# Differential attention scores from two row halves of TensorE without zero padding, with two pairs of score banks in place of three

## The reference

```python
for i in range(S // Q_BLOCK):                       # 8 blocks of 128 queries
    q0 = i * Q_BLOCK
    end = q0 + Q_BLOCK
    s = einsum('bqhmd,bkhmd->bhmqk', q[:, q0:end], k[:, :end]) * scale   # m: two maps, d = 64
    s = s + bias[None, :, None]
    s = where(rel >= 0, s, -inf)
    p = softmax(s, axis=-1)
    a = p[:, :, 0] - lam * p[:, :, 1]
    outs.append(einsum('bhqk,bkhv->bqhv', a, v[:, :end]))
```

## Time and profile before

| | us |
|---|---|
| median of 3 runs | 2963.22 (2961.62 to 2967.35) |
| the profiled execution | 2965.12 |
| its span, first to last instruction | 2963.2 |
| TensorE busy | 2685.0 (91%) |
| VectorE busy | 1151.2 (39%) |
| ScalarE busy | 840.4 (28%) |
| mean granted TensorE clock | 0.964 of full speed |

### The profile page before, as it was taken

The page is one execution under the profiler, slowest core; times in us unless marked ns, Lnnn a source line. Parts: engine busy times, 40 slices in busy tenths (PEclk is TensorE's granted clock), DMA queues, the critical chain, the costliest instruction groups (busy, mean ns, idle before and its releaser), DMA issues. The chain is left out here.

```text
span 2963.2 us, 30511 instructions
## 1 busy us (share of the span) xinstructions
PE 2685.0 (91%) x12386; PEld 2163.3 (73%) x12386; DVE 1151.2 (39%) x1849; ACT 840.4 (28%) x1469; POOL 122.6 (4%) x159
## 2 busy tenths in 40 slices
PE   8789987769999999999989898876899999999997
PEld 7577775447788888878767687644778888887875
DVE  0543444665422221145554434366451111113554
ACT  0421213543311111134542112155341111113333
POOL 0000000002100000001000000000120000000000
PEclk9898998999999999999999989899999999999998
DMA  4242110002322221144445301100131111113444
GB/s 188 87 168 88 29 57 8 1 22 100 100 71 73 72 70 50 50 137 169 149 151 170 128 22 36 36 1 15 57 114 50 50 50 46 47 50 128 164 144 140
DMA packets 171704, 243.60 MB, mean 82 GB/s; under 512 B 9532, under 2 KB 125101, under 8 KB 170541
## 3 DMA queue, kind: packets, MB, share of 16 engines
q1 hardware_dynamic: 160268, 200.74, 21.1%
q0 software_dynamic: 11296, 40.92, 3.9%
HBM read 224.05 MB, written 17.58 MB: 82 GB/s over the span
## 5 line engine op out<-in xcount | busy, mean ns | idle before, releaser
L1643 PE MATMUL ps<-hT,wsp 128*128 128x512 f32 (+1 forms) x1824 | 720.4, 395 | 9.7 <-DVE hT L1471 6.5
L1645 PE MATMUL ps<-hT,wsp 128*128 128x512 f32 (+1 forms) x1824 | 715.6, 392 | 0.0
L1644 PE MATMUL ps<-hT,wsp 128*128 128x512 f32 (+1 forms) x1824 | 715.3, 392 | 0.0
L1029 DVE TENSOR_TENSOR wsp<-raw,wsp 128x1024 fp32r<-128x1024 f32 (+2 forms) x124 | 148.4, 1197 | 959.1 <-ACT wsp L614 731.5
L1643 PEld LDWEIGHTS ps<-hT,wsp 128*128 128x128 f32 (+1 forms) x1824 | 342.8, 188 | 88.5 <-DVE hT L1471 7.6
L1645 PEld LDWEIGHTS ps<-hT,wsp 128*128 128x128 f32 (+1 forms) x1824 | 341.9, 187 | 76.6 <-issue 2.0
L1644 PEld LDWEIGHTS ps<-hT,wsp 128*128 128x128 f32 (+1 forms) x1824 | 342.5, 188 | 74.4 <-issue 1.4
L614 ACT ACTIVATE wsp<-raw 128x1024 fp32r<-128x1024 f32 x84 | 89.1, 1060 | 767.4 <-PE ps L1645 767.4
L1909 PE MATMUL ps<-hT,asp 128*128 128x512 f32 x1032 | 249.0, 398 | 16.5 <-DVE asp L1548 16.3
L1909 PE MATMUL ps<-wsp,asp 128*128 128x512 f32 x1080 | 257.2, 394 | 4.6 <-DVE asp L1548 4.3
L1909 PEld LDWEIGHTS ps<-hT,asp 128*128 128x128 f32 x1032 | 196.1, 191 | 64.2 <-DVE hT L1540 11.0
(11 more groups left out here) (186 smaller groups left out, 2790.4 us busy)
## 6 DMA issues: line engine op xcount, KB each, us to landing
raw<-in_w_down SPq DMA_DIRECT2D x132, 512.0 KB, 3.5
raw<-in_w_gate_up SPq DMA_DIRECT2D x88, 512.0 KB, 3.8
F<-in_w_mod SPq DMA_DIRECT2D x80, 512.0 KB, 4.6
raw<-in_w_in SPq DMA_DIRECT2D x48, 512.0 KB, 3.7
out_x<-W POOLq DMA_DIRECT2D x32, 512.0 KB, 3.4
W<-out_x POOLq DMA_DIRECT2D x24, 512.0 KB, 5.8
raw<-in_w_out SPq DMA_DIRECT2D x16, 512.0 KB, 3.4
F<-in_w_mod SPq DMA_DIRECT2D x6, 1024.0 KB, 18.6
```

The source lines that it names most:

```text
L1029: v.tensor_tensor(wsp[0:np_, r, 1, 0:w], raw[0:np_, r, 0:w], wsp[0:np_, r, 0, 0:w].bitcast(F32), ALU.subtract).then_inc(s_lo, 1)
L1643: mm(o, a(0), b(0), start=start, stop=False)
L1644: mm(o, a(0), b(1), start=False, stop=False)
L1645: return mm(o, a(1), b(0), start=False, stop=stop)
```

## The change

The scores read queries and keys directly from `F`, map 0 from partitions 0-63 and map 1 from partitions 64-127, without the padded copies. `scores(h, b)` issues both maps of a block, piece by piece and alternately: map 0 into `pair(0)`, map 1 into `pair(1)`. The third pair of banks is no longer used for scores. The scores of block b wait until both exponentials of block b - 1 have read the banks. The factor DK ** -0.5 moves into ScalarE's eviction of the projected queries. `queries`, the memsets, `s_q` and `s_qz` go. In the orders of TensorE, ScalarE and VectorE both maps of block b + 1 are handled in block b; `turned(b, 1)` follows `turned(b, 0)` directly. `hi_out` and `lo_out` of tiles 0 and 1 move behind the last head.

```diff
@@ projection, ScalarE
                     nc.scalar.activation(F[:, bass.ds(i * (2 * S) + (Fq + r * S), S)], pair(r),
-                                         ACT.Copy).then_inc(s_tev, 1)
+                                         ACT.Copy, scale=DK ** -0.5 if i < 2 else 1.0).then_inc(s_tev, 1)
@@ ScalarE
-                def queries(h):
-
-                    act.wait_ge(s_qk, 1 + counts(h)[0])
-                    for m in range(2):
-                        rows = slice(DK * m, DK * m + DK)
-                        last = nc.scalar.activation(Wq[m][rows], F[rows, bass.ds(h * S + Fq, S)],
-                                                    ACT.Copy, scale=DK ** -0.5)
-                    last.then_inc(s_q, 1)
-
-                    nc.scalar.activation(F[:, at:at + n], pair(u % 3)[:, 0:n], ACT.Exp,
+                    nc.scalar.activation(F[:, at:at + n], pair(u % 2)[:, 0:n], ACT.Exp,
@@
                         probs(b, 0)
-                        if 2 * b + 3 < 2 * NT:
-                            exps(h, 2 * b + 3)
+                        if b < NT - 1:
+                            exps(h, 2 * b + 2)
                         elif more:
                             exps(h + 1, 0, groups_before(NT - 1) - groups_before(NT))
                         if b >= 4:
                             probs(b, 1)
-                        if 2 * b + 4 < 2 * NT:
-                            exps(h, 2 * b + 4)
+                        if b < NT - 1:
+                            exps(h, 2 * b + 3)
+                        elif more:
+                            exps(h + 1, 1, groups_before(NT - 1) - groups_before(NT))
                         if b:
                             outs(b - 1)
-                        if b == NT - 2 and more:
-                            queries(h + 1)
-                        if b in (1, 2) and not more:
-                            hi_out(b - 1)
-                    if more:
-                        exps(h + 1, 1)
-                        exps(h + 1, 2)
                     outs(NT - 1)
@@
                 head(HEADS - 1, False)
+                hi_out(0)
+                hi_out(1)
                 hi_out(2)
@@ VectorE
-                v.memset(Wq[0][DK:P], 0.0)
-                v.memset(Wq[1][0:DK], 0.0).then_inc(s_qz, 1)
@@
                         combine(b)
-                        for u in (2 * b + 3, 2 * b + 4):
+                        for u in (2 * b + 2, 2 * b + 3):
                             if u < 2 * NT:
                                 maxes(h, u)
-                        if b in (1, 2) and not more:
-                            lo_out(b - 1)
@@
                 v.tensor_scalar(Wf[4], Wf[3], 1.0 / DV, EPS, ALU.mult, ALU.add).then_inc(s_ams, 1)
+                lo_out(0)
+                lo_out(1)
                 lo_out(2)
@@ TensorE
-                def scores(h, u):
+                def scores(h, b):
                     u0 = l * 64 + h * 16
-                    b, m = u // 2, u % 2
                     n = (b + 1) * P
-                    pe.wait_ge(s_ex, 1 + u0 + max(0, u - 2))
+                    pe.wait_ge(s_ex, 1 + u0 + 2 * b)
                     for c0 in range(0, n, 512):
                         w = min(512, n - c0)
-                        last = mm(pair(u % 3)[:, c0:c0 + w], Wq[m][:, b * P:b * P + P],
-                                  F[:, bass.ds(h * S + (Fk + c0), w)],
-                                  start=True, stop=True)
-                    last.then_inc(s_qk, 1)
+                        for m in range(2):
+                            rows = slice(DK * m, DK * m + DK)
+                            last = mm(pair(m)[:, c0:c0 + w],
+                                      F[rows, Fq + h * S + b * P:Fq + h * S + b * P + P],
+                                      F[rows, Fk + h * S + c0:Fk + h * S + c0 + w],
+                                      start=True, stop=True)
+                            if c0 + w == n:
+                                last.then_inc(s_qk, 1)
@@
-                        if 2 * b + 3 < 2 * NT:
-                            scores(h, 2 * b + 3)
+                        if b < NT - 1:
+                            scores(h, b + 1)
+                        elif more:
+                            scores(h + 1, 0)
                         if b:
                             weighted(b - 1)
                         turned(b, 0)
-                        if 2 * b + 4 < 2 * NT:
-                            scores(h, 2 * b + 4)
-                        elif b == NT - 1 and more:
-                            pe.wait_ge(s_q, l * HEADS + h + 2)
-                            scores(h + 1, 0)
-                            scores(h + 1, 1)
                         if b >= 4:
                             turned(b, 1)
-                    if more:
-                        scores(h + 1, 2)
                     weighted(NT - 1)
```

More of the change, by code:

```diff
@@ L209, in build @@
         Ws = [W[:, 4096 + 256 * i:4352 + 256 * i] for i in range(4)]
-        Wq, Wj = [W[:, 0:1024], W[:, 4096:5120]], W[:, 3072:3200]
+        Wj = W[:, 3072:3200]
         Wf = [W[:, 3200 + 32 * z:3232 + 32 * z] for z in range(6)]
@@ L277, in build @@
         s_oh, s_ol = sem("s_oh"), sem("s_ol")
-        s_qz, s_fin = sem("s_qz"), sem("s_fin")
-        s_q, s_qk, s_ba, s_mx = sem("s_q"), sem("s_qk"), sem("s_ba"), sem("s_mx")
+        s_fin = sem("s_fin")
+        s_qk, s_ba, s_mx = sem("s_qk"), sem("s_ba"), sem("s_mx")
         s_ex, s_rc, s_co, s_ad = sem("s_ex"), sem("s_rc"), sem("s_co"), sem("s_ad")
@@ L820, in hi_out @@
                     act.wait_ge(s_raw[n % 2], raw_in(l, n))
-                    if k < 2:
-                        act.wait_ge(s_q, l * HEADS + HEADS)
-                    elif k < 4:
+                    if k < 4:
                         act.wait_ge(s_qk, 1 + l * 64 + 64)
@@ L860, in head @@
                             probs(b, 1)
-                        if 2 * b + 4 < 2 * NT:
-                            exps(h, 2 * b + 4)
+                        if b < NT - 1:
+                            exps(h, 2 * b + 3)
+                        elif more:
+                            exps(h + 1, 1, groups_before(NT - 1) - groups_before(NT))
                         if b:
                             outs(b - 1)
-                        if b == NT - 2 and more:
-                            queries(h + 1)
-                        if b in (1, 2) and not more:
-                            hi_out(b - 1)
-                    if more:
-                        exps(h + 1, 1)
-                        exps(h + 1, 2)
                     outs(NT - 1)
                 act.wait_ge(s_tev, l * 12 + 12)
[L875 to L878, removed]
+                exps(0, 0)
+                exps(0, 1)
                 for h in range(0, HEADS - 1):
@@ L1326, in maxes @@
                     dve.wait_ge(s_qk, 1 + u0 + u + 1)
-                    near = pair(u % 3)[:, n - w:n]
+                    near = pair(u % 2)[:, n - w:n]
                     v.tensor_tensor(near, near, F[:, bass.ds(h * NEAR + (Fbias + NEAR - w), w)],
@@ L1330, in maxes @@
                     dve.wait_ge(s_ba, u0 + u + 1)
-                    v.tensor_reduce(ast[:, A_NM + u:A_NM + u + 1], pair(u % 3)[:, 0:n], AX.X,
+                    v.tensor_reduce(ast[:, A_NM + u:A_NM + u + 1], pair(u % 2)[:, 0:n], AX.X,
                                     ALU.max, negate=True).then_inc(s_mx, 1)
@@ L1363, in head @@
                         combine(b)
-                        for u in (2 * b + 3, 2 * b + 4):
+                        for u in (2 * b + 2, 2 * b + 3):
                             if u < 2 * NT:
                                 maxes(h, u)
-                        if b in (1, 2) and not more:
-                            lo_out(b - 1)
                     if more:
-                        for u in range(3):
+                        for u in range(2):
                             maxes(h + 1, u)
-                for u in range(3):
+                for u in range(2):
                     maxes(0, u)
@@ L1883, in head @@
                         turned(b, 0)
-                        if 2 * b + 4 < 2 * NT:
-                            scores(h, 2 * b + 4)
-                        elif b == NT - 1 and more:
-                            pe.wait_ge(s_q, l * HEADS + h + 2)
-                            scores(h + 1, 0)
-                            scores(h + 1, 1)
                         if b >= 4:
                             turned(b, 1)
-                    if more:
-                        scores(h + 1, 2)
                     weighted(NT - 1)
-                pe.wait_ge(s_q, l * HEADS + 1)
-                for u in range(3):
-                    scores(0, u)
+                pe.wait_ge(s_tev, l * 12 + 12)
+                scores(0, 0)
                 apart(pe)
```

## The result

The changed kernel takes 3023.36 us (median of 4 runs, 3004.08 to 3040.83) where the kernel before took 2965.28 beside it: slower by 58 us, a ratio of 1.0197, 95% interval [1.0137, 1.0257]. The forecast was 3003, own range 2983 to 3028. The profiled execution took 3040.83 us, span 3038.8, at a mean granted clock of 0.925 (before 0.964). The lines of the page that moved are those of the attention.

What follows compares the result with a forecast made beforehand. The attention stage was taken as a chain through three engines, none full. Start -4.5, loop +2.8, last head -6.8, tail +3.7, clock +30 and -5 give +20.2 us a layer, +40 for both: 3003 us, range 2983 to 3028.

Steps and rivals of the forecast that it cites:

- the terms without the clock: Start, loop, last head, tail and the present falls of the clock (-4.5, +2.8, -6.8, +3.7, -5 us a layer).
- The maps at once: Scores: both row halves overlap fully, so 1024 keys cost 1.72 us for both maps and not 3.44.
- the rival without overlap: Scores of both maps stand in line, 49.5 us a head, 3045 us in all; chance 0.13.
- The loop at the full clock: Attention blocks: 43.0 us a head against 42.3 before, 6.5 at block 5, +2.8 us a layer.
- The start: Start of the attention stage: memsets and query copies no longer hold the first score, -4.5 us a layer.
- The last head: Last head: splits of weight tiles 0 and 1 leave its loop, -6.8 us a layer.
- the -5: Clock falls already present in heads 1 and 2 and at the last head's end, subtracted as -5 us a layer.
- The tail: Behind the last head: TensorE waits for the moved weight splits before the output matmuls, +3.7 us a layer.
- The clock: Attention stage: thinner TensorE work lowers the clock, two fifths of it at the low level, +30 us a layer.
- its own price of 72 us: Attention stage at the low clock throughout: four heads at about 18 us, 72 us a layer.
- The rival "the clock holds": Attention clock stays as now, so the change gains -4.8 us a layer, 2954 us; chance 0.12.
- The rival "low through the whole stage": Attention clock low throughout, +72 us a layer and not +30, 3087 us; chance 0.10.

Runs made afterwards that it cites:

- the second set: The changed kernel, unaltered, measured once more with a second profile: 3015.86 us, ratio 1.0181 against the kernel before.
- the filled kernel: Changed kernel plus one useless 512-column matmul behind the transposes of every block: 2936.61 us, ratio 0.9911 against the kernel before.
- e2: Changed kernel's order and two pairs of banks, but with the zero-padded query copies of the kernel before: 3077.79 us, ratio 1.0384.
- e1: Changed kernel plus one useless 512-column matmul behind the transposes of every block: 2936.61 us, ratio 0.9911.
- e8: Changed kernel with the 512-column filler, weight splits of output tiles 0 and 1 moved into block 7 of the last head: 2928.63 us, ratio 0.9881.
- e9: Changed kernel with the useless 512-column matmul behind the transposes of blocks 0 to 3 of each head only: 2962.71 us, ratio 0.9988.
- e3: Kernel before with its three pairs and order, but row-half scores without copies, and splits behind the last head: 3008.52 us, ratio 1.0146.
- e6: Three-pair kernel with row-half scores and no copies, plus a useless matmul ahead of every weighted sum: 2981.1 us, ratio 1.0046.
- e5: Kernel before plus one useless full-array matmul ahead of the weighted sums: 2963.53 us, ratio 0.9995.
- e7: Changed kernel with the 512-column filler, all score pieces of map 0 issued ahead of those of map 1: 2936.09 us, ratio 0.9904.

## Why the prediction was right

The sign and the cause came out as forecast, and the size within its own range of 2983 to 3028: the medians are 3023 and 3016, above the 3003. The loss is 58 us (51 in the second set) where 40 was forecast, and three of the eight executions (3033 to 3041) lie above the range. A little of it is luck: the terms without the clock add up to -9.8 us a layer, and the filled kernel, which is nearly free of the low clock, has -13.6 ((2936.61 - 2963.75) / 2), so they were too high where the clock's term was too low. Step by step:

- **The maps at once**: right. 1.35 us for eight records of 640 keys; the rival without overlap is excluded (e2 shows what it costs, 3.70 us for 1.99).
- **The loop at the full clock**: right, 42.93 us a head for 43.0, and each block within 0.1 us (e1); from weighted sum to weighted sum at block 5 it is 6.68 us (509.18 to 515.86) for 6.5. That the halved scores and the missing lookahead cancel stands: 42.9 us a head for 42.3 before (42.5, when the eight blocks are read to hundredths).
- **The start**: -4.3 us a layer for -4.5.
- **The last head**: in the filled kernel it takes what the other heads take (42.6 us from its first transposes to its end), where before it took 53.3 (621.58 to 674.9): -10.7, for the -6.8 and the 2 of the -5 that lay there.
- **The tail**: +3.8 us a layer for +3.7, for the reason given; e8 takes it out, 7.5 us in all.
- **The clock**: the right mechanism, too small a term. "I take some two fifths of the TensorE work at the low level, +30 us a layer" is the step that was off. The runs gave 33 to 51, with the stage at 0.66 to 0.74 and not 0.75; by its own price of 72 us for a stage that is low throughout that is 0.46 to 0.71 of the work and not 0.4. The prediction read rightly that the small blocks would be thin. What it left out is the feedback: at the low level block 3 takes 8.0 us and not 5.3, TensorE is idle ahead of its scores for the same waits, and the next block starts low as well, heavy ones too. Blocks 4, 5 and 6 of head 0 take 8.18, 9.85 and 7.73 us in the changed kernel; the same blocks, unfilled too, take 6.14, 6.90 and 5.95 in e9, where the blocks ahead of them had kept the clock. With 44 in place of 30 the sum gives 3033 for the profiled executions, which took 3041 and 3015.
- **The rival "the clock holds"** is excluded for this kernel, and e1 shows where it would have ended: 2937 us with the clock held better than now. The Trainium skill (TensorE: Matmul & The Clock Gate, Why this matters for your kernels) warns of long idle gaps between bursts; no gap in the changed loop is longer than 2.5 us, and the clock fell all the same. The measurement decides.
- **The rival "low through the whole stage"** (3087) is excluded: low for 156.6 of 228.7 us, and no execution over 3041.

One cause is shown for the slowdown: adding useless work to TensorE, and nothing else, makes it a gain of 0.9%. The two hybrids show two ways to the same loss: waits thin TensorE's work when the work is as before (e2, two pairs), and the halving does when the lookahead is as before (e3, three pairs). For each I had expected that the other part was needed, and missed. What stays open is why e6 stays low in a full block; rows, changes of form and the state in which the block begins all differ from the kernel before, and no run parts them.

## What to carry to other kernels

In a chain through several engines, a cut of TensorE's work that isn't on the longest path can cost more than it gives, because the work was what kept its clock up: before making matmuls cheaper, look at the granted clock of the stage and at the busy share of its thinnest blocks. A matmul of no use, laid in a wait that is there anyway, is a cheap test of whether the clock is what was lost, and may be the repair; put it in the thinnest blocks first, and price it, since where it stands in line it can take all that the clock gives back (e5). When work is moved out of a loop to its end, look at which engine then waits with nothing in hand.

## What the hardware showed unexpectedly

- TensorE stayed at the low level through a block of 11.9 us in which it was busy without a pause, over half of it score matmuls on 64 rows, one map at a time (e6). In the kernel before, the level came back after such full stretches. A busy engine was not enough here.
- Two row halves run side by side whichever is issued first: 1.35 us with alternate issue, 1.36 us one map after the other (e7), where records of map 1 start ahead of records of map 0 that the program has first. The Trainium skill (TensorEngine Tiling (Array Packing), Key Properties) says that different tiles can execute in parallel; the trace agrees (two records start 0.014 us apart).
- The clock's loss is not the same in two executions of one program: 42.5 and 51.2 us in the stage of layer 0, and the changed kernel scatters over 37 us in its first four executions, where the one before scatters over 6 in four and over 15 in all of its own.
